# Loading x in quarters and transposing it inside two steps, at the head of a two-block fp32 kernel

## What is computed

```python
for l in range(DEPTH):
    h = rmsnorm(x, norm_g[l])          # x: (256, 1024)
    proj = h @ w_in[l]                 # (1024, 4096): q, k, v, gate of both kinds
    ...
    x = x + y @ w_out[l]
return rmsnorm(x, final_g)             # then the second block, much longer
```

## Time and profile before

| | us |
|---|---|
| median of the timed runs | 1205.9 |
| profiled execution, device time | 1205.66 |
| its span on the core | 1203.8 |
| TensorE (PE) busy | 1186.5 |
| TensorE weight loads (PEld) busy | 975.2 |
| VectorE (DVE) busy | 799.3 |
| ScalarE (ACT) busy | 586.5 |
| GpSimd (POOL) busy | 559.6 |

### The profile page before, as it was taken

One profiled execution on the slowest core, in us unless ns is written; L12 is line 12 of the kernel. 1 busy time (PEld: TensorE's weight loads), 2 busy tenths in 40 slices (PEclk: granted clock), 3 DMA queues, 4 the chain that ended last, 5 costly groups with the idle time before them and its releaser, 6 DMA issues.

```text
span 1203.8 us, 15431 instructions
## 1 busy us (share of the span) xinstructions
PE 1186.5 (99%) x5752; PEld 975.2 (81%) x5752; DVE 799.3 (66%) x1118; ACT 586.5 (49%) x764; POOL 559.6 (46%) x418
## 2 busy tenths in 40 slices
PE   8999999999999999899999999999999999999998
PEld 6888888788788888788888888888888887888887
DVE  6885468845787687678768666697673675644423
ACT  5566465665643443454434357444352665534440
POOL 1465334564454443545445226764452464445360
PEclk9999999999999999999999999999999999999999
DMA  9976369845798899459888748798884444766650
GB/s 349 356 273 234 105 237 334 280 163 172 243 342 289 293 343 352 159 164 337 296 311 312 276 175 276 248 330 299 308 295 166 150 154 157 262 215 204 210 192 35
DMA packets 183224, 297.92 MB, mean 247 GB/s; under 512 B 8368, under 2 KB 100208, under 8 KB 183152
## 3 DMA queue, kind: packets, MB, share of 16 engines
q1 hardware_dynamic: 177696, 284.82, 68.4%
q10 hardware_dynamic: 5456, 12.13, 3.0%
HBM read 295.84 MB, written 1.08 MB: 247 GB/s over the span
## 4 chain that ended last, share of the span: by engine, by line
PE 88%; DVE 5%; ACT 2%; POOL 2%; issue 1%; SPq 1%; DMA 1%; ACTq 0%; DVEq 0%
PE ps L1822 26%; PE ps L1835 26%; PE ps L1827 26%; PE ps L2088 2%; PE ps L1849 1%; PE ps L1972 1%; PE ps L1914 1%; PE ps L2000 1%; PE ps L1988 1%; POOL stat L501 1%; DMA raw<-w_in 1%; DVE w_lo L1158 1%; ACT w_hi L641 1%; PE ps L1960 1%; PE ps L2011 1%
## 5 line engine op out<-in xcount | busy, mean ns | idle before, releaser
L510 POOL TENSOR_TENSOR w_lo<-raw,w_hi 128x512 fp32r<-128x512 f32 x348 | 478.6, 1407 | 447.8 <-ACT w_hi L641 447.8
L641 ACT ACTIVATE w_hi<-raw 128x2048 fp32r<-128x2048 f32 x188 | 354.4, 1909 | 103.1 <-PE ps L1835 68.3
L1822 PE MATMUL ps<-w_hi,h_hi 128*128 128x512 f32 x1120 | 313.6, 402 | 1.4 <-issue 0.8
L1835 PE MATMUL ps<-w_lo,h_hi 128*128 128x512 f32 x1120 | 301.4, 391 | 1.4 <-POOL w_lo L510 0.5
L1827 PE MATMUL ps<-w_hi,h_lo 128*128 128x512 f32 x1120 | 300.5, 390 | 0.0
L1158 DVE TENSOR_TENSOR w_lo<-raw,w_hi 128x2048 fp32r<-128x2048 f32 x96 | 224.5, 2342 | 111.8 <-ACT w_hi L641 108.1
L1835 PEld LDWEIGHTS ps<-w_lo,h_hi 128*128 128x128 f32 x1120 | 209.3, 188 | 48.8 <-DVE w_lo L1158 1.7
L1827 PEld LDWEIGHTS ps<-w_hi,h_lo 128*128 128x128 f32 x1120 | 210.2, 188 | 46.0 <-DVE h_lo L1219 0.2
L1822 PEld LDWEIGHTS ps<-w_hi,h_hi 128*128 128x128 f32 x1120 | 200.6, 188 | 44.0 <-issue 6.8
L1144 DVE SCALAR_TENSOR_TENSOR ps<-ada_raw,ccol,ps 128x512 f32<-128x512 f32 x240 | 181.1, 754 | 9.1 <-DMA ada_raw<-ada_w 2.4
L914 ACT ACTIVATE a_hi<-ps 128x512 fp32r<-128x512 f32 x44 | 26.3, 599 | 160.8 <-PE ps L2088 160.8
(11 more groups left out here) (198 smaller groups left out, 979.7 us busy)
## 6 DMA issues: line engine op xcount, KB each, us to landing
raw<-ffn_in SPq DMA_DIRECT2D x176, 512.0 KB, 5.8
ada_raw<-ada_w SPq DMA_DIRECT2D x144, 512.0 KB, 7.3
raw<-ffn_out SPq DMA_DIRECT2D x44, 1024.0 KB, 6.7
raw<-w_in SPq DMA_DIRECT2D x31, 1024.0 KB, 8.5
raw<-w_out SPq DMA_DIRECT2D x8, 1024.0 KB, 6.2
ada_raw<-kv_ada_w SPq DMA_DIRECT2D x16, 512.0 KB, 9.0
raw<-w_kv SPq DMA_DIRECT2D x8, 1024.0 KB, 5.6
bias<-na_bias ACTq DMA_DIRECT2D x16, 256.0 KB, 4.3
```

Source lines behind the costliest of these rows:

```text
L510: ins = pool.tensor_tensor(w_lo[:, u % RAW, piece], raw[:, u % RAW, piece], w_hi[:, u % RING, piece].bitcast(F32), ALU.subtract)
L641: act.activation(w_hi[:, u % RING, :], raw[:, u % RAW, :], ACT.Copy).then_inc(*S.inc("w_hi_ready", u))
L1822: pe.matmul(bank(b), hi[:, k_in_lhs + k, tok], wh[:, k, c * 512:(c + 1) * 512], start=start and k == 0, stop=False)
L1835: ins = pe.matmul(bank(b), hi[:, k_in_lhs + k, tok], wl[:, k, c * 512:(c + 1) * 512], start=False, stop=stop and k == nk - 1)
```

## The change

Three things are moved at the head of the kernel.

The loads: x comes in four quarters of 256 KB (token tile by channel half), each with a semaphore of its own. The first quarter goes ahead of unit 0, and the other three behind both of its halves, in the order tile 1 half 0, tile 0 half 1, tile 1 half 1. The identity and the norm columns get a semaphore each, so that TensorE waits for the identity only, and ScalarE and VectorE for the columns.

The transposes: only tile 0 half 0 is transposed before step 0, tile 1 half 0 between the products of step 0, and half 1 of both tiles between the products of step 1. In the two steps of unit 0 the run of low products is made chunk pair by chunk pair, behind the high products of the same pair. The warm-up is two products instead of three.

The order on the engines: ScalarE makes the high part of unit 1 between the two tiles' half 1 of `h_hi`, and unit 2 before the first square; VectorE makes the low part of unit 1 between the two tiles' half 1 of `h_lo`.

```diff
-WARM_UP = (3, 1)
+WARM_UP = (2, 1)
...
-            sp.dma_start(x[:, 0, :], x_in[0:P, :]).then_inc(x_in_sem[0], 16)
+            def load_x(t, half):
+                cols = slice(512 * half, 512 * half + 512)
+                sp.dma_start(x[:, t, cols], x_in[t * P:(t + 1) * P, cols]).then_inc(x_in_sem[t][half], 16)
+
+            load_x(0, 0)
...
                 if u == 0:
-                    sp.dma_start(x[:, 1, :], x_in[P:2 * P, :]).then_inc(x_in_sem[1], 16)
+                    for t, half in ((1, 0), (0, 1), (1, 1)):
+                        load_x(t, half)
...
-            for into, src in first_consts:
-                act.dma_start(into, src).then_inc(first_in, 16)
+            act.dma_start(ident[:], identity).then_inc(ident_in, 16)
+            act.dma_start(gcols[:], norm_cols).then_inc(gcols_in, 16)
...
                 done[0] = 1
-                act.wait_ge(first_in, N_FIRST)
+                act.wait_ge(gcols_in, 16)
                 for t in range(NT):
+                    if t:
+                        fill(1)
                     act.wait_ge(*S.at("xT_done", "a0", t, 1))
...
-                fill(1)
+                fill(2)
                 act.wait_ge(*S.at("stat_filled"))
                 for t in range(NT):
-                    act.wait_ge(x_in_sem[t], 16)
+                    for half in range(2):
+                        act.wait_ge(x_in_sem[t][half], 16)
                     act.activation(hn[:, t, :], x[:, t, :], ACT.Square, accum_out=st(t)).then_inc(
                         *S.inc("squares_ready", "a0", t))
-                    fill(2 + t)
-                fill(4)
+                    fill(3 + t)
...
                 for t in range(NT):
                     first_low(t, 1)
-                lows(2)
+                    lows(1 + t)
...
-            dve.wait_ge(first_in, N_FIRST)
+            dve.wait_ge(gcols_in, 16)
...
-                for k in range(nk):
-                    if u == 0 and k == nk // 2:
+                for part in (range(0, nk // 2), range(nk // 2, nk)) if u == 0 else (range(nk),):
+                    if u == 0 and part[0]:
                         pe.wait_ge(*S.at("w_hi_ready", 0))
-                    for c, b in enumerate(banks):
-                        pe.matmul(bank(b), hi[:, k_in_lhs + k, tok], wh[:, k, c * 512:(c + 1) * 512],
-                                  start=start and k == 0, stop=False)
-                lhs_wait(lo_ready)
-                for k in range(nk):
-                    for c, b in enumerate(banks):
-                        pe.matmul(bank(b), lo[:, k_in_lhs + k, tok], wh[:, k, c * 512:(c + 1) * 512],
-                                  start=False, stop=False)
+                    for k in part:
+                        for c, b in enumerate(banks):
+                            pe.matmul(bank(b), hi[:, k_in_lhs + k, tok], wh[:, k, c * 512:(c + 1) * 512],
+                                      start=start and k == 0, stop=False)
+                    lhs_wait(lo_ready)
+                    for k in part:
+                        for c, b in enumerate(banks):
+                            pe.matmul(bank(b), lo[:, k_in_lhs + k, tok], wh[:, k, c * 512:(c + 1) * 512],
+                                      start=False, stop=False)
                 between()
...
+            def raw_T(t, half):
+                pe.wait_ge(x_in_sem[t][half], 16)
+                transpose_half("a0", t, half, "xT_done")
...
-            pe.wait_ge(first_in, N_FIRST)
+            pe.wait_ge(ident_in, 16)
             for layer in range(DEPTH):
                 name = f"a{layer}"
                 if layer == 0:
-                    norm_T(name, 0)
+                    raw_T(0, 0)
                     warm_up(WARM_UP[1])
...
                 def between(s):
                     if s == 0 and not layer:
-                        norm_T(name, 1)
+                        raw_T(1, 0)
+                    if s == 1 and not layer:
+                        raw_T(0, 1)
+                        raw_T(1, 1)
```

More of the change, by code:

```diff
@@ L335, in program @@
         bias_in = [ctx.enter_context(nc.semaphore(f"bias_in{i}")) for i in range(BIASES)]
-        x_in_sem = [ctx.enter_context(nc.semaphore(f"x_loaded{t}")) for t in range(NT)]
+        x_in_sem = [[ctx.enter_context(nc.semaphore(f"x_loaded{t}_{half}")) for half in range(2)] for t in range(NT)]
         ROWS = {("down", 0, 0): 2, "pool": 5, "pool_scale": 4, "pool_shift": 3, ("down", 0, 1): 8,
@@ L344, in program @@
         half_in = ctx.enter_context(nc.semaphore("first_half_loaded"))
-        first_in = ctx.enter_context(nc.semaphore("first_constants_loaded"))
+        ident_in = ctx.enter_context(nc.semaphore("identity_loaded"))
+        gcols_in = ctx.enter_context(nc.semaphore("norm_columns_loaded"))
         const_in = ctx.enter_context(nc.semaphore("constants_loaded"))
@@ L349, in program @@
         out_sem = ctx.enter_context(nc.semaphore("out_stored"))
-        first_consts = [(ident[:], identity), (gcols[:], norm_cols)]
         consts = [(bcols[:], ada_b_cols),
@@ L353, in program @@
                   (lamr[:], lam_rows), (qk_norm[:], qk_rows), (trig[:], rope)]
-        N_FIRST, N_CONST = 16 * len(first_consts), 16 * len(consts)
+        N_CONST = 16 * len(consts)
         def bank(b, n=1):
@@ L1917, in norm_T @@
             def norm_T(name, t, hat=None):
-                if name == "a0":
-                    pe.wait_ge(x_in_sem[t], 16)
                 for half in range(2):
-                    transpose_half(name, t, half, "xT_done", [("x_hat_ready", hat or name, t)] if name != "a0" else ())
+                    transpose_half(name, t, half, "xT_done", [("x_hat_ready", hat or name, t)])
+            def raw_T(t, half):
+                pe.wait_ge(x_in_sem[t][half], 16)
+                transpose_half("a0", t, half, "xT_done")
             def mix_part(half, to, of):
```

## The result

The changed kernel takes 1208.74 us (median, 1207.99 to 1210.39) against 1205.93 for the kernel before, measured beside it: ratio 1.0024, interval 1.0017 to 1.0031, so it is slower by about 2.8 us. The profiled execution took 1209.22 us with a span of 1207.2.

The account below looks back on a forecast made before the run. TensorE was taken to bound the kernel after 30 us; ScalarE, VectorE and loads bound the head. A 0.4 us load gain and ScalarE's wait summed to +2.7 us on 1205.9, forecasting 1208.6 us, range 1206.4 to 1210.4.

Parts of the forecast that it names:

- the case that carried it: Head: ScalarE idle behind the moved transposes delays unit 1 and all behind it; 1208.3 to 1209.4 us, chance 0.47.
- Gain of the loads: Ahead of unit 0: 256 KB less of x in front gains 0 to 0.65 us, taken as 0.4.
- ScalarE's first high part near 6.7: Sign at unit 0: a start near 6.7 us would show the load step is right.
- My upper bound of 0.65: Loads ahead of unit 0: 256 KB less at 402 GB/s gains 0.65 us at most.
- GpSimd's block: Unit 0's first-half low part on GpSimd: program unchanged, so the low weights' product moves only from 11.98 to 11.58.
- case B: Head: delay partly absorbed as GpSimd's long piece returns from 2.36 to 1.29 us; 1206.5 to 1208.2, chance 0.27.
- The second step: TensorE's second step: starts at 12.39, products take 1.83 us, moved transposes start at 14.22.
- Marks: Head: unit 1's high part near 16.0, third step near 20.3, first query transposes near 32.7 with about 0.8 us wait.
- the same distance at every later mark: After the first query group's transposes: the 2.7 us delay stays unchanged, as TensorE has no idle time there.
- Case D: Head: shorter warm-up or TensorE's new gaps leave it at 1.2 GHz, or VectorE is pushed further; 1210.4 at worst, chance 0.16.
- Case A: Head: unit 4's landing keeps pacing it, so ScalarE's wait is free; 1205.9, down to 1205.3, chance 0.08.
- Cutting x at no cost: Loads: two more SP issues ahead of unit 1 cost nothing; uncovered, up to about 0.4 us each.

Follow-up runs that it names:

- the two orders mended: Changed kernel with unit 1's high part before ScalarE's half 1 scalings and its low part before VectorE's half 1 low parts of h: 1207.39 us, ratio 1.0014.
- the 1.0014: Kernel before with each token tile of x loaded as two 256 KB pieces, same queue places, waited for together: 1207.15 us, ratio 1.0014.

## Why the prediction was right, and where it was not

The time, 1208.74, is next to the forecast 1208.6, and the case that carried it is the one that happened: ScalarE idle behind the moved transposes. The moved transposes alone cost 4.8 us in the kernel before, and putting them back takes 1.5 us (medians) to 2.4 us (marks) off the changed kernel. With the two orders mended, 1.8 us of the marks return. But the closeness is luck in part, since it hides terms that were mis-sized and that cancelled: the distance at the query transposes came out 0.46 us smaller than the forecast's, and later additions, of which the granted clock is the larger, were not in the sum. In executions without a drop the changed kernel takes 1208.1.

- *Gain of the loads*: 0.4 us in the sum, 1.83 at the low weights' product (11.98 to 10.15). The sign that I gave for this step, ScalarE's first high part near 6.7, failed: it started at 5.13. Of this, 0.9 is the late start of the profile of before (7.11 against 6.20). Over all profiles, that part starts at 5.13 to 5.56 in the eight kernels with the quarter in front and at 6.11 to 6.33 in four of the five with the whole tile; the medians are 5.41 and 6.20, so the change itself gave about 0.8. My upper bound of 0.65, from bytes over rate, was too low, since the ramp counted too: the whole tile landed 3.8 to 4.0 us after its issue (4.8 in the first profile of before), the quarter after 2.7 to 2.9. The Trainium skill ("DMA: Bandwidth & Descriptors", Anatomy of one DMA) gives an estimated 0.60 for the same term by its rate of 436 GB/s; it fits that to DMAs issued by GpSimd, these are issued by SP, and it is no nearer.
- *GpSimd's block*: I let its second piece take 2.36 us again. The two pieces took 2.51 together, since VectorE's subtraction began at 8.75, when GpSimd was nearly done. That is the condition of my case B, and the start of TensorE's product did come earlier. In this profile nothing holds that product: the subtraction has ended at 9.97, and it begins right behind the four transposes (from 9.80 on). In the second profile of the change the subtraction ends at 10.35 and the product begins at 10.50.
- *The second step*: I had no wait in it. VectorE was late with tile 1's half 0, and TensorE waited for h_hi (0.30 us before its weight load at 11.18) and 0.43 us for h_lo, which the order by pairs asks for after two products instead of four. The transposes' weight loads started at 13.61, forecast 14.22: of 1.43 us of lead beyond the forecast (11.58 to 10.15), 0.61 was left.
- *Marks*: unit 1's high part 16.00 forecast, 15.56 measured; third step 20.29 and 19.86; query transposes 32.7 and 32.26, with a TensorE wait of 0.27 us instead of 0.8. All 0.4 us early, all in the order told. The distance of 2.7 us to the profile of before was 2.24.
- *After 33 us*: "the same distance at every later mark" failed. 0.17 us came before 100 us, and 0.9 at the mixer, from the granted clock. The larger part of the 0.17 lies between the transposes near 80 and near 121 us, which are 41.29 to 41.38 us apart in all eight profiles of kernels built on the changed one and 41.17 or 41.18 in the six built on the kernel before, the one with moved transposes among them; so it does not come from the transposes. I have no cause for it.
- *Case D*: a TensorE wait in the head with a drop behind it shows in the variant with only the transposes moved, not in the two profiles of the change. It may have come in some of the timed executions: the four of the changed kernel at a mean clock of 0.997 took 1208.82 to 1210.39 us (median 1209.89). Where their second slow stretch lies, no profile shows. I had not looked at the mixer at all.
- *Case A* rested on unit 4's landing as what paces the head. It holds in the first profile of before and with all transposes in step 0 (waits of 0.48 and 1.15 us), not in the second profile of before.
- *Cutting x at no cost* was wrong: 1.7 us in the kernel before. The version with quarters and all transposes in step 0 is about 1 us above before, which I put down to the same cause; no run separates it. The Trainium skill's rule of one DMA and not several ("SBUF — State Buffer", rules for kernel authors), which I had set aside for want of a row, is borne out here by the 1.0014.

The balance of the change, from marks and against the second profile of before: 32.26 - 29.25 = 3.0 us, of which 2.4 go with the place of the transposes and 0.6 remain with them in step 0.

## What to carry to other kernels

When work is moved later on the engine that seems to have time, look in every other engine's program at what stands behind the instruction that waits for it; an engine that runs in order makes everything behind that instruction late too. A load gained at the front is only worth what the next thing in line lets through, and cutting a load in pieces has a price of its own. And take a second profile of the kernel before: one execution's start of the loads was 0.9 us from the other's, a third of the whole effect. Where the mean granted clock of each execution is on record, compare executions with the same one.

## What the runs showed of the hardware

- TensorE's granted clock drops to the 1.2 GHz level at the pooling mixer in 8 of 14 profiles, behind the same wait of 2.3 us, and costs 0.7 to 1.0 us by the marks ahead of and behind it. The same wait left it at 2.4 GHz in the other six, both of the kernel before among them; but 31 of 97 timed executions of that kernel have a mean clock that only profiles with a drop show. So a kernel with such a wait has two times.
- A wait of 2.86 us in the head was followed by the drop, one of 1.83 us was not, in one and two profiles.
- At the start of the kernel a TensorE instruction can take double its later time while the granted clock reads 1.00 (the first product of step 0: 0.94 to 1.18 us in four profiles, 0.47 to 0.67 in ten).
- While pieces of x of 256 KB came in between 6 and 7 us, the loads moved 209 to 236 GB/s in six profiles; with both tiles whole, 387 to 420 in five.
- The loads come up to rate at different moments in executions of one kernel (250 or 399 GB/s between 3 and 4 us).
